# Dilated attention by even and odd query tokens: 128 keys of one parity per dilated group, one PSUM bank per head

## The chip, the cores and the metric

The program runs on one core of one Trainium2 chip. The metric is the device time of one launch in microseconds (us), here the median of three runs.

## The reference

Two layers (DEPTH 2) of a decoder trunk on 256 tokens of width 1024, all in float32. Each layer projects the normed residual with one wide matrix, runs four attention branches (A, B, C, M), gates and mixes them, and ends in an MLP. The change is in branch C, dilated attention with 8 heads of width 64 in three groups:

```python
C_PATTERNS = ((128, 1), (512, 4), (2048, 16))
for g, (win, dil) in enumerate(C_PATTERNS):
    cq, ck, cv = c_parts[3 * g:3 * g + 3]
    qc = apply_rope(rms_norm(cq.reshape(B, S, C_HEADS, C_HD), c_qn[l, g]), cos_h, sin_h)
    kc = apply_rope(rms_norm(ck.reshape(B, S, C_HEADS, C_HD), c_kn[l, g]), cos_h, sin_h)
    o_g, lse_g = dilated_group(qc, kc, vc, win, dil)
wts = jax.nn.softmax(jnp.stack(lses, axis=0), axis=0)
o_c = jnp.einsum('gbsh,gbshd->bshd', wts, jnp.stack(outs, axis=0))
```

In `dilated_group` position t attends t - m*dilation, for m from 0 to window//dilation. In the groups with dilation 4 and 16 an even token therefore sees only even tokens and an odd one only odd tokens. The weighting of the three groups by their denominators is the same as one softmax over the keys of all three.

## The kernel before

Every weight matrix is streamed from HBM in units of up to 256 rows by 512 columns (`unit`). SyncE issues the load into `raw`, ScalarE (ACT) rounds it to `w_hi` (L937), VectorE (DVE) writes the rest to `w_lo` (L1103), and TensorE (PE) does three matmuls for each 128 rows and 128 tokens: L1366, L1367 and L1368. This stream of weight matmuls fills most of PE's time. Everything else is put between them.

The order on each engine comes from a planner. `plan` makes a list of items with costs, needs and a wish for their place (`order`), and `arrange` places them engine by engine. The engines then run their lists in order and wait on semaphores. Four banks of PSUM (`ps_b`) serve all transposes, scores and outputs of attention. An item that needs banks waits until they are empty.

Branch C in the kernel before, for each layer, each block of 128 query tokens (tt 0 and 1) and each pair of heads (`head_steps`):

- scores, L1415: three items, one per group. Each does one float32 matmul for each head of the pair, with the 64 rows of the head's width as contraction and 128 keys (tt 0) or 256 keys (tt 1). The two heads lie in different halves of the rows. Each item takes two banks.
- mask, L1282: one DVE instruction per head and group adds the mask, negates and keeps the running minimum in `part_top` and, for the last group, `neg_top`. A second short instruction reads the minimum out.
- exp, L1051 on ACT, over 384 or 768 elements a row; then reciprocal and scaling on DVE, L1289 and L1290.
- transposes of the probabilities on PE, L1421: 3 blocks of 128 keys per head in tt 0, and 6 in tt 1 (two items of 4 and 2); each item is copied out by ACT (L1025).
- values, L1443: one item per pair, 3 or 6 key blocks for each of the two heads, summed in one bank.

Queries and keys come to `q_c` and `k_c` by PE transposes (L1395) and ACT evictions (L1009). The last of them is the second eviction of group 2's keys, which the first complete set of scores waits for. Values come straight from the projection in PSUM to `v_c` by ACT (L1040, `copyv`). L1068 is the issue of the gate bias loads from ACT's queue. `home_of` gives places in `q_c` and `k_c` that branch B's tokens borrow before branch C needs them.

Of the kernel before, what the change touches and what calls it, by code (L numbers as in the profile page):

```python
# [7 lines left out]
P = 128  # L8
# [23 lines left out]
assert S == 2 * P and all(d == 1 or d * P >= S for d in DILATION)  # L32
# [6 lines left out]
P_RING, PT_RING = {"C": 2, "": 4}, 2  # L39
# [11 lines left out]
        ("C", 0): (P + 2 * S, C_G * P), ("C", 1): (P + 2 * S + C_G * P, C_G * S)}  # L51
MASK_W = P + 2 * S + C_G * (P + S)
# [89 lines left out]
def plan():  # L142
# [4 lines left out]
         "v": 0, "ready": 0, "pv": 0, "osplit": 0,  # L147
# [135 lines left out]
    def turn(source, came, c, m, width, dest, mode="plain", gain=None, l=0, order=None, since=0.0, **k):  # L283
# [18 lines left out]
        lay = left_homes.get(dest, []) if c == 0 else []  # L302
        soon = (axis[0] if order is None else order) - 3.0
        e = item("evict", "ACT", cost, [t] + lay, order=soon, chain="", lay=lay, of=t, dest=dest, mode=mode, gain=gain, c=c, m=m, width=width, l=l)
# [36 lines left out]
    def copy_values(job, dest, factor, takes):  # L341
        v = count("v")
        it = item("copyv", "ACT", 1.3 if factor else 0.6, [job.last, factor_at.get(factor)], job=job, dest=dest, factor=factor, v=v,
                  takes=takes, root=factor_at.get(factor))
        values_at[dest] = it
        if takes:
            job.taken = it
        return it

    values_at = {}  # L350
# [4 lines left out]
    def head_steps(l, branch, hs, tt, heads):  # L355

        sts, masks_of = [], []
        for h in hs:
# [3 lines left out]
            blocks = TT if branch == "M" else tt + 1  # L362
            st = dict(ring=ring, slot=len(mine) % P_RING[ring], s=s, branch=branch, h=h, tt=tt, blocks=blocks,
                      gs=C_G if branch == "C" else 1, l=l, before=mine[-P_RING[ring]] if len(mine) >= P_RING[ring] else None,
# [12 lines left out]
            masks_of.append([])  # L377
        dests = {"A": ("qA", "kA"), "M": ("qM", "kM"), "B": ("qB%d" % (hs[0] // 4), "kB%d" % (hs[0] // 4))}.get(branch)
        for g in range(sts[0]["gs"]):
            ds = dests or ("qC%d" % g, "kC%d" % g)  # L380
            cost = 4 * sts[0]["blocks"] * P / 2400 * (2 if branch == "B" else 1) + (0.25 if branch in "AC" else 0.15)
            sc = item("scores", "PE", cost, [o for d in ds for o, _ in plain_turns[d]], sts=sts, g=g,
                      turns=[t for d in ds for _, t in plain_turns[d]])
            sc.opens = len(sts)
            for d in ds:
                plain_last.setdefault(d, []).append(sc)
            for n_in, st in enumerate(sts):
                before = st["before"]
                mk = item("mask", "DVE", dve_cost(st["blocks"] * P) + 0.15,
                          [sc] + (before["turns"] if before else []) + (held["heads"] if branch == "C" else []),  # L390
                          st=st, g=g, of=sc, at=n_in, e=count("tile"), pv=held["heads"][0] if branch == "C" else None,
                          last_part=masks_of[n_in][-1] if g else None)
                sc.closed_by.append(mk)
                masks_of[n_in].append(mk)
        copies = []
        for st, own in zip(sts, masks_of):
            gs, blocks = st["gs"], st["blocks"]
            ex = item("exp", "ACT", act_cost(gs * blocks * P, 1) + 0.2, [own[-1]], st=st, tile=own[-1])
            nm = item("pnorm", "DVE", 0.2 + dve_cost(gs * blocks * P), [ex], st=st)
            st["turns"] = []  # L400
            free_at = st["pt_before"]["pv"] if st["pt_before"] else None
            for b in range(0, gs * blocks, 4):
                m = min(4, gs * blocks - b)
                pt = item("pturn", "PE", 0.06 + 0.108 * m, [nm], st=st, c=b, m=m)
                pt.opens = 1
                pc = item("pcopy", "ACT", act_cost(m * P), [pt, free_at], chain="pcopy", of=pt, st=st, c=b, m=m, pv=free_at)
                pt.closed_by = [pc]
                st["turns"].append(pt)
                copies.append(pc)
        first, i = sts[0], sts[0]["i"]  # L410
        vs = {"A": ("vA",), "M": ("vM",), "B": ("vB%d" % (first["h"] // 4),)}.get(branch, ("vC0", "vC1", "vC2"))
        pv = item("pv", "PE", 0.22 * first["gs"] * first["blocks"] + 0.2, copies + [values_at[v] for v in vs], sts=sts,
# [53 lines left out]
    for l in range(DEPTH):  # L466
# [22 lines left out]

        aq = w_in(COL["aq"], BW, part=(0, half), fine=l == 0)  # L490
# [6 lines left out]
        copy_values(j, "vC1", "mix", True)  # L497
# [24 lines left out]
        copy_values(j, "vC2", "mix", True)  # L522
# [129 lines left out]
def hybrid_block(nc, x, mem, positions, inv_freq, g_mix, w_in, b_gate, a_qn, a_kn, a_sink, b_qa_norm, b_kva_norm,  # L652
# [32 lines left out]
    with ExitStack() as ctx:  # L685
# [32 lines left out]
        neg_top, part_top = sb("neg_top", [P, TOPS]), sb("part_top", [P, 2, C_G])  # L718
# [25 lines left out]
        prob_c = part(2 * C_G).rearrange("p (i c) -> p i c", i=2)  # L744
        probT_c = part(2 * C_G).rearrange("p (i c) -> p i c", i=2)
# [4 lines left out]
        ang, trig = start[:, 5 * S + 128:5 * S + 128 + TT * FREQ], start[:, 6 * S:6 * S + 2 * TT * FREQ]  # L750
        exps = {b: (prob_c, probT_c) if b == "C" else (prob[:], probT[:]) for b in "ABCM"}
# [4 lines left out]
        values = {"vA": v_a, "vM": v_m, "vC0": v_c[:, 0], "vC1": v_c[:, 1], "vC2": v_c[:, 2]}  # L756
# [17 lines left out]
        prob_scaled = sem("prob_scaled")  # L774
# [25 lines left out]

        def home_of(home):

            place = tok[:, home] if home in (0, 1) else (q_c if home[0] == "q" else k_c)[:, int(home[2])].rearrange("p c s -> p (c s)")
            return place.rearrange("p (t c) -> p t c", t=TT)
# [56 lines left out]
        def _(pool):  # L861
# [21 lines left out]
            for it in placed["POOL"]:  # L883
# [16 lines left out]
                elif it.kind == "selects":  # L900
                    pool.wait_ge(dve_const, 1)
                    chains = []
                    for (branch, tt), (m0, w) in MASK.items():
                        if (branch, tt) == ("B", 0):
                            continue
                        keys = (tt + 1) * P
                        for g in range(w // keys):
                            cut = mask[:, m0 + g * keys:m0 + (g + 1) * keys]
                            chains.append((cut, dict(base=tt * P, pattern=[[-1, keys]], channel_multiplier=1), 0))
                            reach = P - 1 if branch == "A" else P if branch == "C" and g == 0 else S  # L910
                            if reach < (tt + 1) * P - 1:
                                chains.append((cut, dict(base=reach - tt * P, pattern=[[1, keys]], channel_multiplier=-1), 1))
# [8 lines left out]
        def _(act):  # L921
# [7 lines left out]
            for it in placed["ACT"]:  # L929
# [62 lines left out]
                elif it.kind == "evict":  # L992
# [12 lines left out]
                    if a["mode"] == "plain":  # L1005
# [3 lines left out]
                        nc.scalar.activation(plain[a["dest"]][0:wd, c:c + m], src, ACT.Copy, scale=scale).then_inc(bank_free[b], 1)  # L1009
# [9 lines left out]
                elif it.kind == "pcopy":  # L1019
                    t, st, m, c = a["of"], a["st"], a["m"], a["c"]  # L1020
# [4 lines left out]
                    nc.scalar.activation(exps[st["branch"]][1][:, st["pt_slot"], c * P:(c + m) * P], ps_b[:, b, 0:m * P],  # L1025
                                         ACT.Copy).then_inc(bank_free[b], 1)
                elif it.kind == "copyv":
# [9 lines left out]
                    act.wait_ge(root_ready, a["root"].a["q"] + 1)  # L1037
                    of = ps_d[:, j % 2, :, P:2 * P] if dest == "vA" else ps_d[:, j % 2]
                    for tt in range(TT):
                        last = nc.scalar.activation(values[dest][:, tt], of[:, tt], ACT.Copy, scale=factor[a["factor"]][:, tt:tt + 1])  # L1040
                    last.then_inc(v_ready if dest == "vA" else set_free[j % 2], 1)
                elif it.kind == "loadmem":
# [4 lines left out]
                elif it.kind == "exp":  # L1047
                    st = a["st"]
                    act.wait_ge(masked, a["tile"].a["e"] + 1)
                    p = prob_of(st)[:, 0:st["gs"] * st["blocks"] * P + (st["branch"] == "A")]  # L1050
# [37 lines left out]
        def _(dve):  # L1088
# [8 lines left out]
            for it in placed["DVE"]:  # L1097
# [40 lines left out]
                elif it.kind == "masks":  # L1138
                    dve.wait_ge(pool_const, 1)
                    for g, dil in enumerate(DILATION):  # L1140
                        if dil == 1:
                            continue
                        rest = rests[g]
                        link(nc.vector.tensor_scalar(rest, dist, dil - 1, None, ALU.bitwise_and))
                        for tt in range(TT):
                            m0, keys = MASK["C", tt][0], (tt + 1) * P
                            last = nc.vector.tensor_scalar(mask[:, m0 + g * keys:m0 + (g + 1) * keys], rest[:, 0:keys], 0.0, NEG,
                                                           ALU.not_equal, ALU.mult)
                        link(last)
# [103 lines left out]
                elif it.kind == "mask":  # L1253
                    st, g, t = a["st"], a["g"], a["of"]
# [12 lines left out]
                    else:  # L1267
                        m0 = MASK[branch, tt][0] + g * keys
# [7 lines left out]
                    elif g:  # L1276
                        dve.wait_ge(masked, a["last_part"].a["e"] + 1)
                        first = part_top[:, st["s"] % 2, g - 1:g]
                    else:
                        first = -NEG  # L1280
                    top = top_of(st) if g == st["gs"] - 1 else part_top[:, st["s"] % 2, g:g + 1]
                    nc.vector.tensor_tensor_reduce(prob_of(st)[:, g * keys:(g + 1) * keys], ps_b[:, b, 0:keys], cut,  # L1282
                                                   -(1.0 if branch in "AC" else SCALE[branch]), first, ALU.add, ALU.min,
                                                   top).then_inc(masked, 1)
# [188 lines left out]
```

## Time and profile before

| | |
|---|---|
| median of three runs | 1224.99 us (1223.71 to 1227.89) |
| profiled execution | 1222.76 us |
| its span, first to last instruction | 1221.0 us |
| PE busy | 1208.7 us |
| DVE busy | 832.0 us |
| ACT busy | 701.0 us |
| granted TensorE clock | 1.00 |
| bytes moved by DMA | 202.60 MB |

Busy time of PE counts overlapped matmuls once, so it tells that PE had work and not how fast that work went. The cost of an item on PE is read from the chain of waits, in which the pieces follow one another without overlap.

### The profile page before, as it was taken

How to read it: one execution, taken by the hardware profiler on the slowest of the kernel's cores; microseconds unless marked ns; L12 is line 12 of the kernel's file. 1: busy time of each engine (PE TensorE's matmuls, PEld its weight loads, DVE VectorE, ACT ScalarE, POOL GpSimd, SP SyncE). 2: the span in 40 equal slices, each digit the busy share in tenths (PEclk: the TensorE clock that was granted, in tenths of full speed). 3: DMA queues.
4: the chain of work that ended last, by engine and by line, in shares of the span. 5: the costliest groups of instructions: out<-in, count | busy, mean ns of one | idle time of the engine just before them, and what ended most of it. 6: DMA issues, size and time to landing. Idle time of an engine off the chain costs nothing.

```text
span 1221.0 us, 17637 instructions
## 1 busy us (share of the span) xinstructions
PE 1208.7 (99%) x6232; PEld 979.9 (80%) x6232; DVE 832.0 (68%) x1447; ACT 701.0 (57%) x1079; POOL 145.9 (12%) x127
## 2 busy tenths in 40 slices
PE   8999999999999999999999999999999999999998
PEld 7888787777778888888888878877777788888887
DVE  5868889886766764544567688798877667554444
ACT  5666766645554465455566677666555544645553
POOL 5511322210000000000021223322000000000000
PEclk9999999999999999999999999999999999999999
DMA  9655444465447556666656444545545566566563
GB/s 253 192 142 159 138 121 136 137 202 157 146 137 223 176 176 187 188 187 184 192 160 188 136 146 138 140 138 165 163 130 153 158 188 183 174 188 183 181 188 103
DMA packets 111220, 202.60 MB, mean 166 GB/s; under 512 B 10016, under 2 KB 18720, under 8 KB 111136
## 3 DMA queue, kind: packets, MB, share of 16 engines
q1 hardware_dynamic: 106128, 194.64, 53.6%
q10 hardware_dynamic: 4464, 6.82, 1.8%
q8 instruction: 52, 0.85, 0.3%
q0 software_dynamic: 544, 0.03, 0.1%
q14 instruction: 32, 0.26, 0.1%
HBM read 200.41 MB, written 1.05 MB: 165 GB/s over the span
## 4 chain that ended last, share of the span: by engine, by line
PE 97%; DMA 2%; ACT 1%; issue 0%; DVE 0%; ACTq 0%; DVEq 0%
PE ps_d L1366 24%; PE ps_d L1368 22%; PE ps_d L1367 22%; PE ps_b L1366 5%; PE ps_b L1368 5%; PE ps_b L1367 5%; PE ps_b L1415 4%; PE ps_b L1395 4%; PE ps_b L1443 3%; PE ps_b L1421 2%; DMA raw<-in_w_in_dram 1%; DMA early<-in_mem_dram 1%; ACT w_hi L937 0%; ACT k_c L1009 0%; DVE w_lo L1103 0%
## 5 line engine op out<-in xcount | busy, mean ns | idle before, releaser
L1103 DVE TENSOR_TENSOR w_lo<-raw,w_hi 128x1024 fp32r<-128x1024 f32 (+4 forms) x381 | 451.2, 1189 | 277.0 <-ACT w_hi L937 276.0
L937 ACT ACTIVATE w_hi<-raw 128x1024 fp32r<-128x1024 f32 (+4 forms) x381 | 391.3, 1027 | 421.6 <-PE ps_d L1368 315.5
L1366 PE MATMUL ps_d<-w_hi,h_hi 128*128 128x512 f32 (+3 forms) x704 | 283.8, 403 | 1.4 <-DVE w_lo L1103 0.9
L1368 PE MATMUL ps_d<-w_hi,h_lo 128*128 128x512 f32 (+3 forms) x704 | 267.7, 380 | 0.0
L1367 PE MATMUL ps_d<-w_lo,h_hi 128*128 128x512 f32 (+3 forms) x704 | 267.0, 379 | 0.0
L1366 PE MATMUL ps_d<-w_hi,r_hi 128*128 128x512 f32 (+1 forms) x552 | 219.9, 398 | 0.0
L1368 PE MATMUL ps_d<-w_hi,r_lo 128*128 128x512 f32 (+1 forms) x552 | 214.2, 388 | 0.0
L1367 PE MATMUL ps_d<-w_lo,r_hi 128*128 128x512 f32 (+1 forms) x552 | 214.0, 388 | 0.0
L1366 PEld LDWEIGHTS ps_d<-w_hi,h_hi 128*128 128x128 f32 x704 | 132.4, 188 | 33.3 <-issue 10.3
L1368 PEld LDWEIGHTS ps_d<-w_hi,h_lo 128*128 128x128 f32 x704 | 132.2, 188 | 25.2
L1367 PEld LDWEIGHTS ps_d<-w_lo,h_hi 128*128 128x128 f32 x704 | 132.8, 189 | 19.3
L1366 PEld LDWEIGHTS ps_d<-w_hi,r_hi 128*128 128x128 f32 x552 | 103.7, 188 | 23.7 <-issue 3.5
L1368 PEld LDWEIGHTS ps_d<-w_hi,r_lo 128*128 128x128 f32 x552 | 103.6, 188 | 21.2
L889 POOL TENSOR_TENSOR root<-sums,power 128x16 f32<-128x16 f32 (+3 forms) x32 | 86.5, 2702 | 274.6 <-DVE sums L1179 232.2
L1367 PEld LDWEIGHTS ps_d<-w_lo,r_hi 128*128 128x128 f32 x552 | 103.8, 188 | 19.0
L1366 PE MATMUL ps_b<-w_hi,h_hi 128*128 128x512 f32 x256 | 101.1, 395 | 0.0
L1367 PE MATMUL ps_b<-w_lo,h_hi 128*128 128x512 f32 x256 | 99.7, 390 | 0.0
L1368 PE MATMUL ps_b<-w_hi,h_lo 128*128 128x512 f32 x256 | 99.7, 389 | 0.0
L1368 PEld LDWEIGHTS ps_b<-w_hi,h_lo 128*128 128x128 f32 x256 | 48.1, 188 | 10.0
L1366 PEld LDWEIGHTS ps_b<-w_hi,h_hi 128*128 128x128 f32 x256 | 48.1, 188 | 9.9 <-issue 0.5
L1367 PEld LDWEIGHTS ps_b<-w_lo,h_hi 128*128 128x128 f32 x256 | 48.1, 188 | 9.4
L889 POOL TENSOR_TENSOR factor_mlp<-sums,power 128x1 f32<-128x1 f32 x4 | 2.2, 557 | 379.4 <-DVE sums L1188 379.4
(158 smaller groups left out, 1239.9 us busy)
## 6 DMA issues: line engine op xcount, KB each, us to landing
raw<-in_w_in_dram SPq DMA_DIRECT2D x151, 512.0 KB, 3.7
raw<-in_w_up_dram SPq DMA_DIRECT2D x64, 512.0 KB, 3.7
raw<-in_w_down_dram SPq DMA_DIRECT2D x64, 512.0 KB, 4.0
raw<-in_w_branch_dram SPq DMA_DIRECT2D x32, 512.0 KB, 3.7
raw<-in_m_w_kv_dram SPq DMA_DIRECT2D x16, 512.0 KB, 4.5
raw<-in_w_out_dram SPq DMA_DIRECT2D x16, 512.0 KB, 3.7
early<-in_b_gate_dram ACTq DMA_DIRECT2D x16, 256.0 KB, 3.6
raw<-in_w_in_dram SPq DMA_DIRECT2D x8, 384.0 KB, 3.8
```

The source lines that it names most:

```text
L889: nc.gpsimd.tensor_tensor(to, sums[:, slot, 0:w], power[:, 0:w], ALU.pow).then_inc(root_ready, 1)
L937: nc.scalar.activation(w_hi[:, u % RING, 0:kn, 0:cn], raw[:, u % RAW, 0:kn, 0:cn], ACT.Copy).then_inc(hi_split, 1)
L1103: nc.vector.tensor_tensor(w_lo[:, u % RING, 0:kn, 0:cn], raw[:, u % RAW, 0:kn, 0:cn], w_hi[:, u % RING, 0:kn, 0:cn].bitcast(F32), ALU.subt ...
L1366: nc.tensor.matmul(o, hi[:, a["c"], cut], wh, start=a["first"], stop=False)
L1367: nc.tensor.matmul(o, hi[:, a["c"], cut], wl, start=False, stop=False)
L1368: last = nc.tensor.matmul(o, lo[:, a["c"], cut], wh, start=False, stop=a["last"])
L1395: last = nc.tensor.transpose(ps_b[0:wd, b, k * P:(k + 1) * P], v, ident[:])
L1415: nc.tensor.matmul(ps_b[:, b, 0:keys], q, k, start=True, stop=True).then_inc(bank_full[b], 1)
L1421: last = nc.tensor.transpose(ps_b[:, b, k * P:(k + 1) * P], prob_of(st)[:, c * P:(c + 1) * P], ident[:])
L1443: last = nc.tensor.matmul(ps_b[r0:r0 + d, b, c:c + P], v[:, b2, vh * d:(vh + 1) * d], pT[:, k * P:(k + 1) * P], start=k == 0, stop=k == le ...
```

## The change

Query block tt now means the tokens of parity tt: even tokens in the first block, odd tokens in the second.

- The eviction of `q_c` (all groups) and of `k_c` (groups 1 and 2) reads PSUM with a stride of two and writes even tokens first and odd tokens behind (`sides`). Keys of group 0 stay in order of time.
- A head has four blocks of keys in either query block: two for group 0 (all 256 keys) and one for each dilated group (128 keys of its parity). The scores of all three groups are one item, fill one bank (512 columns), and have one mask instruction of 512, one exp of 512, one scaling of 512, one transpose item of four blocks and one copy.
- The three scores items of a pair become one, whose matmuls go group by group and, in a group, head by head.
- Values of groups 1 and 2 have to lie by parity on the partitions. `copyv` writes them to a borrowed place (`q_c` or `k_c` of group 0), and four DMAs from ACT's queue (`vmove`) carry each to `v_c`: 64 partitions of 512 values each. The eviction that next writes the borrowed place waits for them, and so does the first values item of each query block.
- The masks are rebuilt for the new layout, `o_c` is written with a stride of two by `oevict`, and the ring of probabilities of branch C holds 4 heads and not 2.

```diff
-P_RING, PT_RING = {"C": 2, "": 4}, 2
+P_RING, PT_RING = {"C": 4, "": 4}, 2
...
+        if stage:
+            values_at[dest] = moved[stage] = item("vmove", "ACT", 1.5, [(it, 0.3)], job=job, dest=dest, stage=stage, k=count("move"))
...
-            blocks = TT if branch == "M" else tt + 1
+            blocks = {"M": TT, "C": C_BLOCKS}.get(branch, tt + 1)
...
-        for g in range(sts[0]["gs"]):
-            ds = dests or ("qC%d" % g, "kC%d" % g)
...
+        ds = {"A": ("qA", "kA"), "M": ("qM", "kM"), "B": ("qB%d" % (hs[0] // 4), "kB%d" % (hs[0] // 4))}.get(
+            branch, tuple(n_ + "C%d" % g for g in range(C_G) for n_ in "qk"))
...
+                        if a["dest"] in sides:
+                            to, src = sides[a["dest"]][:, c:c + m], src.rearrange("p c (i t) -> p c t i", t=TT)
+                        if a["moved"] is not None:
+                            at = a["moved"].a["k"]
+                            act.wait_ge(v_moved[at % 2], 16 * 2 * TT * (at // 2 + 1))
...
+                elif it.kind == "vmove":
+                    job, g = a["job"], int(a["dest"][2])
+                    act.wait_ge(set_free[job.j % 2], set_value(job))
+                    of = home_of(a["stage"])
+                    for half in range(2):
+                        for tt in range(TT):
+                            act.dma_start(v_c[half * P // 2:(half + 1) * P // 2, g, tt], of[tt::TT, half]).then_inc(v_moved[a["k"] % 2], 16)
...
+                    parts = [(0, slice(0, full))] if branch != "C" else [(0, slice(0, S))] + [(g, qs) for g in range(1, C_G)]
+                    at_col = 0
+                    for g, ks in parts:
+                        wide = ks.stop - ks.start
+                        for st, b in zip(a["sts"], it.banks):
...
+                    if branch == "C":
+                        vs = [v_c[:, 0, t2] for t2 in range(TT)] + [v_c[:, g, tt] for g in range(1, C_G)]
```

PE's order around the first scores of branch C in the first layer, before (`ps_b<-k_c,q_c` are scores, `ps_b<-ident,tok` transposes of queries and keys, `ps_d` weight matmuls; an order row x2 of float32 is four records of the trace):

```order
L1395 MATMUL ps_b<-ident,tok 128x128 [waits tok_ready,masked]
L1395 MATMUL ps_b<-ident,tok 128x128 x3
L1415 MATMUL ps_b<-k_c,q_c 128x128 [waits bank_free1,bank_free0,bank_free3,bank_free2,masked]
L1415 MATMUL ps_b<-k_c,q_c 128x128
L1415 MATMUL ps_b<-k_c,q_c 128x128 [waits bank_free1,bank_free2,bank_free0]
L1415 MATMUL ps_b<-k_c,q_c 128x128
L1366 MATMUL ps_d<-w_hi,h_hi 128x512 [waits lo_split,bank_free0,set_free0]
```

The same place on PE in the changed kernel:

```order
L1414 MATMUL ps_b<-ident,tok 128x128 [waits tok_ready,bank_free1]
L1414 MATMUL ps_b<-ident,tok 128x128 x3
L1438 MATMUL ps_b<-k_c,q_c 128x256 [waits bank_free3,bank_free1,bank_free2,bank_free0]
L1438 MATMUL ps_b<-k_c,q_c 128x256
L1438 MATMUL ps_b<-k_c,q_c 128x128 x4
L1385 MATMUL ps_d<-w_hi,h_hi 128x512 [waits lo_split,bank_free0,set_free0]
```

Before, the scores of groups 0 and 1 of the first pair stood earlier, and here came group 2's and the next pair's first. Now all six matmuls of the first pair stand here, behind the last transpose of keys. The next pair's scores follow 12 weight matmuls later, and the first transposes of probabilities 6 after that:

```order
L1438 MATMUL ps_b<-k_c,q_c 128x256 [waits bank_free3,bank_free1,bank_free2,bank_free0]
L1438 MATMUL ps_b<-k_c,q_c 128x256
L1438 MATMUL ps_b<-k_c,q_c 128x128 x4
L1385 MATMUL ps_d<-w_hi,h_hi 128x512 [waits lo_split,bank_free1]
...
L1446 MATMUL ps_b<-ident,early 128x128 [waits prob_scaled,masked]
L1446 MATMUL ps_b<-ident,early 128x128 x3
```

On ACT, the place where the first values are moved, in the changed kernel (the row with `q_c<-ps_d` is the copy to the borrowed place, the DMA rows are `vmove`):

```order
L1055 ACTIVATE q_c<-ps_d,factor_mix 128x512 [waits root_ready,unit_done]
L1055 ACTIVATE q_c<-ps_d,factor_mix 128x512
L944 ACTIVATE w_hi<-raw 128x1024 [waits unit_done,raw_landed1]
L1063 DMA v_c<-q_c 64x512 [waits set_free0]
L1063 DMA v_c<-q_c 64x512 x3
L944 ACTIVATE w_hi<-raw 128x1024 [waits unit_done,raw_landed2]
```

Before, the two roundings to `w_hi` stood next to each other there; now the four DMA issues lie between them.

## Rows read from the trace of the kernel before

**Rows 1.** The page: busy time by engine, and the chain that ended last by engine.

```profile
PE 1208.7 (99%) x6232; PEld 979.9 (80%) x6232; DVE 832.0 (68%) x1447; ACT 701.0 (57%) x1079; POOL 145.9 (12%) x127
...
PE 97%; DMA 2%; ACT 1%; issue 0%; DVE 0%; ACTq 0%; DVEq 0%
```

**Rows 2.** Waits of PE, whole span: us in total, times, longest.

```profile
PE ps_b L1415 <- ACT k_c L1009: 2.8, 2, 1.4
PE ps_b L1395 <- DMA xs<-in_x_dram: 2.7, 1, 2.7
```

**Rows 3.** Busy time by stage: branch C of either layer, and the stretch of the first move.

```profile
257.00:372.00 115.00, 113.60 (x661) 86.06 (x660) 84.03 (x180) 61.87 (x95) 0.00 (x0) 1.00 0.52 151
860.00:975.00 115.00, 113.60 (x660) 86.13 (x659) 83.85 (x178) 61.88 (x95) 0.00 (x0) 1.00 0.52 151
50.00:60.00 10.00, 10.00 (x66) 8.98 (x65) 7.28 (x12) 8.06 (x14) 0.94 (x3) 1.00 0.87 297
```

**Rows 4.** Chain of waits, query block 0: start, us, what, records.

```profile
259.53 0.83 PE ps_b L1415 x8
260.36 0.43 PE ps_d L1366
...
266.51 0.23 PE ps_d L1368
266.75 0.81 PE ps_b L1443 x12
267.56 0.42 PE ps_b L1415 x4
267.98 0.43 PE ps_d L1366
```

**Rows 5.** Chain of waits, query block 1.

```profile
304.94 1.06 PE ps_b L1415 x8
...
308.94 0.63 PE ps_b L1415 x4
...
313.90 0.66 PE ps_b L1421 x6
...
318.64 1.46 PE ps_b L1443 x24
```

**Rows 6.** PE's groups of branch C, shapes apart: records, busy us, mean ns.

```profile
L1421 PE MATMUL ps_b<-ident,early 128*128 128x128 f32 x144 | 19.9, 272 | 0.0
L1443 PE MATMUL ps_b<-early,v_c 128*64 128x128 f32 x288 | 19.3, 278 | 0.0
L1415 PE MATMUL ps_b<-k_c,q_c 64*128 64x256 f32 x96 | 16.3, 424 | 0.0
L1415 PE MATMUL ps_b<-k_c,q_c 64*128 64x128 f32 x96 | 11.5, 321 | 2.8 <-ACT k_c L1009 2.8
```

**Rows 7.** DVE's groups: masks of 128 and 256, scaling of 768, rounding of weights.

```profile
L1282 DVE CUSTOM_DVE_ANT_0 early<-ps_b,mask 128x256 f32<-128x256 f32 x16 | 6.1, 419 | 0.6 <-PE ps_b L1415 0.6
L1282 DVE CUSTOM_DVE_ANT_0 early<-ps_b,mask 128x128 f32<-128x128 f32 x16 | 4.3, 286 | 3.2 <-PE ps_b L1415 2.9 <-issue 0.3
L1290 DVE TENSOR_SCALAR early<-early,den 128x768 f32<-128x768 f32 x16 | 9.9, 621 | 0.6
L1103 DVE TENSOR_TENSOR w_lo<-raw,w_hi 128x1024 fp32r<-128x1024 f32 x347 | 424.7, 1227 | 257.8 <-ACT w_hi L937 256.8
```

**Rows 8.** ACT's groups: exp of 768, evictions of keys.

```profile
L1051 ACT ACTIVATE early<-early,neg_top 128x768 f32<-128x768 f32 x16 | 14.8, 930 | 3.7 <-DVE neg_top L1282 3.6
L1009 ACT ACTIVATE k_c<-ps_b 128x512 f32<-128x512 f32 x12 | 6.9, 590 | 1.9 <-PE ps_b L1395 1.9
```

**Rows 9.** Issues of the bias loads on ACT's queue (ns min/median/max), and their landing.

```profile
L1068 ACTq DMA_DIRECT2D early<-in_b_gate_dram x16: 334/334/335, 238.6 to 972.5; - x16
...
DMA to landing us min/median/max: 3.0/3.6/5.1
```

**Rows 10.** Where the first move falls, in order of time: ACT, DVE and PE.

```profile
51.67 1.06 ACT L937 ACTIVATE w_hi<-raw 128x1024 fp32r<-128x1024 f32 x1 [0.31 <-DMA raw<-in_m_w_kv_dram]
...
52.77 1.23 DVE L1103 TENSOR_TENSOR w_lo<-raw,w_hi 128x1024 fp32r<-128x1024 f32 x1 [0.15 <-ACT w_hi L937]
...
57.47 0.39 PE L1366 MATMUL ps_d<-w_hi,r_hi 128*128 128x512 f32 x1
```

More of the change, by code:

```diff
@@ L31 @@
 N_IN = COL["gate"] + 4 * D
-assert S == 2 * P and all(d == 1 or d * P >= S for d in DILATION)
+assert S == 2 * P and DILATION[0] == 1 and all(d % TT == 0 and d * P >= S for d in DILATION[1:])
+C_BLOCKS = TT + C_G - 1
 UC, NW = 2, 512
@@ L302, in turn @@
         lay = left_homes.get(dest, []) if c == 0 else []
+        came_from = moved.pop(dest, None)
         soon = (axis[0] if order is None else order) - 3.0
-        e = item("evict", "ACT", cost, [t] + lay, order=soon, chain="", lay=lay, of=t, dest=dest, mode=mode, gain=gain, c=c, m=m, width=width, l=l)
+        e = item("evict", "ACT", cost, [t, (came_from, 3.0) if came_from else None] + lay, order=soon, chain="", lay=lay, moved=came_from, of=t, dest=dest, mode=mode, gain=gain, c=c, m=m, width=width, l=l)
         out = e
@@ L339, in plan, with copy_values @@
     factor_at = {}
[L341 removed]
+    def copy_values(job, dest, factor, takes, stage=None, after=None):
         v = count("v")
[L343 removed]
+        it = item("copyv", "ACT", 1.3 if factor else 0.6, [job.last, factor_at.get(factor), after], job=job, dest=dest, factor=factor, v=v, after=after,
                   takes=takes, root=factor_at.get(factor))
@@ new lines, in head_steps @@
+        ds = {"A": ("qA", "kA"), "M": ("qM", "kM"), "B": ("qB%d" % (hs[0] // 4), "kB%d" % (hs[0] // 4))}.get(
+            branch, tuple(n_ + "C%d" % g for g in range(C_G) for n_ in "qk"))
+        cost = 4 * sts[0]["blocks"] * P / 2400 * (2 if branch == "B" else 1) + (0.25 if branch in "AC" else 0.15)
+        sc = item("scores", "PE", cost, [o for d in ds for o, _ in plain_turns[d]], sts=sts,
+                  turns=[t for d in ds for _, t in plain_turns[d]])
+        sc.opens = len(sts)
+        for d in ds:
+            plain_last.setdefault(d, []).append(sc)
@@ L395, in head_steps @@
+        for n_in, st in enumerate(sts):
+            before = st["before"]
+            mk = item("mask", "DVE", dve_cost(st["blocks"] * P) + 0.15,
+                      [sc] + (before["turns"] if before else []) + (held["heads"] if branch == "C" else []),
+                      st=st, of=sc, at=n_in, e=count("tile"), pv=held["heads"][0] if branch == "C" else None)
+            sc.closed_by.append(mk)
+            masks_of.append(mk)
         copies = []
         for st, own in zip(sts, masks_of):
-            gs, blocks = st["gs"], st["blocks"]
@@ L398, in head_steps @@
-            ex = item("exp", "ACT", act_cost(gs * blocks * P, 1) + 0.2, [own[-1]], st=st, tile=own[-1])
-            nm = item("pnorm", "DVE", 0.2 + dve_cost(gs * blocks * P), [ex], st=st)
+            blocks = st["blocks"]
+            ex = item("exp", "ACT", act_cost(blocks * P, 1) + 0.2, [own], st=st, tile=own)
+            nm = item("pnorm", "DVE", 0.2 + dve_cost(blocks * P), [ex], st=st)
             st["turns"] = []
             free_at = st["pt_before"]["pv"] if st["pt_before"] else None
[L402 to L409, printed above, removed]
+            pt = item("pturn", "PE", 0.06 + 0.108 * blocks, [nm], st=st, m=blocks)
@@ new lines, in _ @@
+                    for k, v in enumerate(vs):
+                        for st in sts:
+                            h = st["h"]
+                            vh, r0, c = h // (A_H // A_KV) if branch == "A" else h, h * d % P, h * d // P * P
+                            pT = exps[branch][1][:, st["pt_slot"]]
+                            last = nc.tensor.matmul(ps_b[r0:r0 + d, b, c:c + P], v[:, vh * d:(vh + 1) * d],
+                                                    pT[:, k * P:(k + 1) * P], start=k == 0, stop=k == blocks - 1)
```

176 lines of the change are left out of this document (85 added, 91 removed).

## The prediction

> **What bounds the kernel now.** I read the page first. PE is busy for 1208.7 of 1221.0 us, and the chain that ended last is PE for 97% [rows 1]. Next the waits of PE. Once the program has started, PE waits for another engine for little more than 2.8 us, twice 1.4 us, before the scores of branch C that need the last eviction of keys [rows 2]. Then the stages. In branch C of either layer PE is busy for 113.6 of 115 us, DVE for 84 and ACT for 62, at clock 1.00 [rows 3]. So the time is the sum of what PE's instructions take one behind the other. A change that takes work from PE shortens the program by just that, as long as no new wait appears; work taken from DVE and ACT is worth nothing by itself. The price of an item on PE is its piece in the chain, where nothing overlaps. The mean durations of the groups overlap (272 ns for a transpose that advances the chain by 0.11) and serve here only for counts.
>
> **Scores.** A pair's item costs 0.42 us with 128 keys [rows 4] and 0.63 with 256 [rows 5]. The counts are 96 records of either width, four to an item, so 24 items of each [rows 6]. Two items of 256 back to back take 1.06, so the second adds only 0.43: the item has about 0.2 us of fixed cost, and then runs at its columns [rows 5]. Before: 24 x 0.42 + 24 x 0.63, less 0.4 for the two pairs of items that follow each other with 256 keys, is 24.8 us. After: 16 items, each with one 256-key part (0.63) and two 128-key parts behind it without a semaphore between. This continuation with 128 keys is not in the trace. From below it costs half of 0.43, or 0.22. The values items say the same: 12 more records add 1.46 - 0.81 = 0.65, or 0.22 per four [rows 4, 5]. From above it costs 0.41, since the one place where two 128-key items stand together took 0.83 [rows 4]. There the second item has waits of its own, and inside the new item there are none, so I take 0.22, and keep 0.41 for the range. After: 16 x (0.63 + 0.44) = 17.1. Gain: 7.7 us.
>
> By the page "TensorE: Matmul & The Clock Gate" of the Trainium skill, section on the mechanism of packing, a load of weights overlaps matmuls in flight only when the row group differs. In the new item the next group's weights go to the same rows as the matmuls before them, so the rule speaks for the upper price. The values items load to all 128 rows each time and still advance by 0.22 per four records [rows 4, 5], against the rule, and this row decides.
>
> **Values.** 8 items of 12 records and 8 of 24, 288 in all [rows 6], take 8 x 0.81 + 8 x 1.46 = 18.2 us [rows 4, 5]. After there are 16 items of 16 records, at 0.81 + 0.22 = 1.03, or 16.4. Gain: 1.7.
>
> **Transposes of probabilities.** 144 records [rows 6] at 0.66 / 6 = 0.11 [rows 5] become 8 x 16 = 128. Gain: 1.8.
>
> **Returns to the weight stream.** A weight matmul takes 0.23 in the chain, but 0.43 right behind scores or values of 64 rows or columns [rows 4]. Behind a transpose it doesn't. In the order of instructions 46 such items of branch C are followed by a weight matmul before, and 32 after (16 scores, 16 values). 14 fewer at 0.20: gain 2.8.
>
> The sum is 7.7 + 1.7 + 1.8 + 2.8 = 14.0 us.
>
> **What costs nothing, and under what cover.** On DVE six masks of a head become two of 512. The step from 128 to 256 adds 133 ns [rows 7], so 512 take about 0.69. The exp of 512 and the scaling of 512 are below the 0.93 and 0.62 of the 768-wide ones [rows 7, 8]. These aren't PE's time; they matter only if transposes come before their probabilities. For the first pair: mask and readout 0.8, exp and readout 0.9, reciprocal and scaling 0.7, handovers 0.3, a rounding of weights in the way 1.23 [rows 7], 3.9 in all. PE has 12 weight matmuls (3.0 with 0.2 for the return), the next pair's scores (1.07) and 6 more (1.6), some 5.6 us, before it wants them. Margin 1.7 us. The initial wait of 1.4 before the first scores stays, because the same last eviction releases them [rows 2]. The evictions now read with a stride of two, which no row shows. I take their 0.59 as it is [rows 8]. At twice that, two of them ahead of the first scores would add 1.2 us in each layer, 2.4 in all. Less than 0.59 I exclude, since the elements stay the same. The masks are built long before the first use, and the strided `oevict` is four instructions.
>
> **The moves of values.** 16 DMAs of 128 KB. An issue holds ACT's queue for 0.33 us [rows 9], so each group of four holds it for 1.3. Queued behind them is the next rounding to `w_hi`, then DVE, then PE. In the first layer this falls where DMA engines are already 0.87 busy with 297 GB/s [rows 3], and 512 KB more are 1.8 us at that rate. The load of weights that follows is rounded at 51.67, its rest is done at 54.00, and PE takes it at 57.47 [rows 10]: 3.5 us of margin against 1.3 + 1.8 = 3.1. So I charge 0. If both add up and the planner's small shifts eat the rest, PE waits up to 1.5 us in each layer. The moved values themselves are wanted more than 30 us after their issue; a bias load lands after 3.6, at most 5.1 [rows 9].
>
> From the profiled execution: 1222.76 - 14.0 = 1208.8. The median of the runs shown is 2.2 higher, from which the same sum gives 1211.0. I take the middle, **1209.8**. A measurement of this kernel tells a difference of about 0.3% (3.7 us) from none.
>
> **The rivals.**
>
> *The short parts of the scores don't run on* (0.41 each, as in [rows 4]). For it: the only pair of 128-key items in the trace, and the rule above. Against it: the values items at the same width. 32 parts cost 0.19 more each, 6.1 us: **1215.9**. Chance 0.12.
>
> *The moves and evictions come through*: PE waits where the moves collide with the weight loads (up to 3.0 in both layers), and the strided evictions lengthen the first wait (up to 2.4). For it: ACT and DMA are full at that place. Against it: the margin of 3.5. About half of both is 2.7: **1212.5**, at most 1215.2. Chance 0.10.
>
> *The gain is eaten*: the new order puts transposes of probabilities ahead of their time, and PE waits 0.4 us before each of the 32 items in the two layers, some 13 us: **1222**, within 0.3%. For it: the margin at DVE is the thinnest there. Against it: no transposes item is in the list of waits now [rows 2], and the worked margin is 1.7. Chance 0.05.
>
> *Slower: the mask of a full bank becomes the bound.* One mask now has to be done before anything of a head goes on, and a pair's second mask stands behind the first. If the 512-wide mask takes much longer than 0.69, PE waits before the transposes of each pair. To lose, the 16 pairs have to give back 14.0 + 3.7 = 17.7 us, 1.1 each, on top of the margin of 1.7. It decides from two masks that take 2.8 us more together, 2.1 us for one. At 2.6 us each the waits are 16 x 2.1 = 34: **1243**. Against it: 286 and 419 ns at 128 and 256 columns are a straight line [rows 7]. Chance 0.03.
>
> **How the numbers follow.** The forecast has 0.70. It and the first two rivals are faster by over 0.3%: 0.92. Within 0.3%: 0.05. Slower: 0.03. The lower end is the forecast from the profiled time less the 2.8 us of first waits that a shifted order could hide: 1206.0. The upper end is the rival of the short parts with one more us of waits: 1217.0. What lies above is 0.08 and a part of the middle cases.
>
> **What would show each step.** In the chain of the changed kernel a scores item of branch C with 12 records is one piece of 1.07 us (1.45 if the rival holds); a values item of 16 records is 1.03; a transposes item of four is 0.44; weight matmuls behind them 0.43. Records: 64 of 256 keys and 128 of 128 keys, 256 for values, 128 for transposes. PE's waits stay below 10 us with 1.4 twice before scores. The mask takes 0.69, the evictions of queries and keys 0.59. PE's busy time is some 14 us lower. Wrong would be: new waits of PE on `prob` scaling or on `w_lo` near 55 and 650 us, scores items above 1.2 us, or a busy time of PE that did not fall.

## The result, and the profile after

| | before | changed |
|---|---|---|
| median | 1224.43 us (1223.71 to 1227.89, 4 runs) | 1210.2 us (1209.3 to 1211.05, 4 runs) |
| ratio | | 0.9878, 95% interval 0.9857 to 0.99 |
| span of the profiled execution | 1221.0 us | 1208.7 us |

The change makes the kernel 14.2 us faster (12.2 to 17.5 by the interval); 14.0 was worked out, and 1209.8 forecast. The page of the profile after the change (busy time by engine, then the chain by engine; before: [rows 1]):

```profile
PE 1196.8 (99%) x6184; PEld 980.9 (81%) x6184; DVE 819.7 (68%) x1319; ACT 694.6 (57%) x1063; POOL 142.6 (12%) x128
...
PE 98%; DMA 1%; ACT 0%; issue 0%; ACTq 0%; DVE 0%
```

PE is as full as it was, and busy for 11.9 us less. PE's waits (before: [rows 2]):

```profile
PE ps_b L1414 <- DMA xs<-in_x_dram: 3.7, 1, 3.7
PE ps_b L1438 <- ACT k_c L1022: 2.8, 2, 1.4
PE ps_d L1357 <- POOL ident L870: 1.6, 1, 1.6
PE ps_d L1385 <- ACT q_c L997: 0.5, 2, 0.3
```

The two waits of 1.4 us before the first scores are still there, as forecast, and no new one came. The chain of waits shows the items of branch C in the first layer (before: [rows 4, 5]; start, us, what, records):

```profile
260.96 1.15 PE ps_b L1438 x12
262.11 0.43 PE ps_d L1385
...
307.53 1.08 PE ps_b L1438 x12
308.61 0.43 PE ps_d L1385
...
314.28 0.44 PE ps_b L1446 x4
...
317.94 1.02 PE ps_b L1473 x16
```

A scores item is one piece of 1.08 us (1.07 forecast; the first of each layer, behind its wait, takes 1.15), a values item 1.02 (1.03), four transposes 0.44 (0.44), and the weight matmul behind scores or values 0.43. PE's groups, shapes apart, give the counts (before: [rows 6]), and DVE's and ACT's the new widths (before: [rows 7, 8]):

```profile
L1446 PE MATMUL ps_b<-ident,early 128*128 128x128 f32 x128 | 17.2, 272 | 0.0
L1473 PE MATMUL ps_b<-early,v_c 128*64 128x128 f32 x256 | 17.5, 279 | 0.0
L1438 PE MATMUL ps_b<-k_c,q_c 64*128 64x256 f32 x64 | 11.2, 427 | 2.8 <-ACT k_c L1022 2.8
L1438 PE MATMUL ps_b<-k_c,q_c 64*128 64x128 f32 x128 | 9.8, 271 | 0.0
```

```profile
L1299 DVE CUSTOM_DVE_ANT_0 early<-ps_b,mask 128x512 f32<-128x512 f32 x32 | 20.8, 687 | 10.3 <-PE ps_b L1438 10.3
```

```profile
L1073 ACT ACTIVATE early<-early,neg_top 128x512 f32<-128x512 f32 x32 | 22.9, 717 | 25.4 <-DVE neg_top L1299 25.4
L1022 ACT ACTIVATE k_c<-ps_b 128x512 f32<-128x512 f32 x12 | 6.9, 589 | 1.9 <-PE ps_b L1414 1.9
L1022 ACT ACTIVATE q_c<-ps_b 128x512 f32<-128x512 f32 x12 | 6.7, 591 | 1.1 <-PE ps_b L1414 1.1
```

The mask takes 687 ns, on the straight line through 286 and 419, and the strided evictions take the same 0.59 us as before. (The row of `k_c` mixes both kinds: only group 0's keys, four of the twelve evictions, are read with a stride of one. The twelve lie between 573 and 600 ns.)

The two profiled spans differ by 12.3 us, not by 14.2, because this execution started later: the first weight matmul begins at 11.40 us before and at 14.76 here (timeline of PE, before first):

```profile
11.40 0.48 PE L1366 MATMUL ps_d<-w_hi,h_hi 128*128 128x512 f32 x1
```

```profile
10.58 1.11 PE L1414 MATMUL ps_b<-ident,xs 128*128 128x128 f32 x4 [3.74 <-DMA xs<-in_x_dram]
11.49 3.62 PE L1357 MATMUL ps_d<-ident 128*128 128x128 f32 x16
14.76 0.78 PE L1385 MATMUL ps_d<-w_hi,h_hi 128*128 128x512 f32 x1
```

Here PE stood idle for the input for 3.74 us and not 2.68, and then its 16 dummy transposes took 3.62 us against 1.91. The granted clock (the number before the last two of each row) tells why: from 10 to 15 us it was 1.00 before and 0.50, the level of 1.2 GHz, in the changed kernel (busy time by stretch, PE first; one row of before, then two of the changed kernel):

```profile
10.00:15.00 5.00, 5.00 (x34) 4.42 (x32) 2.91 (x4) 3.62 (x5) 5.00 (x8) 1.00 1.15 213
```

```profile
5.00:10.00 5.00, 1.84 (x14) 1.60 (x12) 1.83 (x4) 1.36 (x3) 5.00 (x8) 0.90 1.02 312
10.00:15.00 5.00, 4.42 (x21) 4.42 (x22) 2.50 (x5) 3.27 (x5) 5.00 (x8) 0.50 1.17 216
```

The same split runs through all profiled executions. Where the clock stayed at 1.00 in this stretch (before and four of the versions below), the first weight matmul begins between 11.4 and 12.3 us; where it was between 0.50 and 0.70 (the changed kernel and six versions), between 13.1 and 16.7. What decides between the two isn't shown: PE had waited 1.6 to 3.6 us for the input in the first group and 2.6 to 5.9 in the second.

A measure free of the start is the distance between the first scores of branch C in the two layers: 862.42 - 259.53 = 602.89 us before, 856.34 - 260.96 = 595.38 after. That is 7.5 us for one layer, 15.0 for two, 1.0 more than the 14.0 worked out. Of this, 0.5 is a wait of some 0.3 us in each layer that before has and the changed kernel hasn't; the rest is not assigned. It stands in the list of PE's waits before:

```profile
PE ps_b L1443 <- ACT probT L1025: 0.5, 2, 0.3
```

### The profile page after: what moved, and what is told of

Same layout as the page of the kernel before. It is cut to its first block, busy times and chain, and to the rows that moved or that the text cites. A ratio compares the mean times of both kernels' runs of the same rounds, so it can differ in the third digit from the quotient of the medians.

```text
span 1208.7 us, 17209 instructions
## 1 busy us (share of the span) xinstructions
PE 1196.8 (99%) x6184; PEld 980.9 (81%) x6184; DVE 819.7 (68%) x1319; ACT 694.6 (57%) x1063; POOL 142.6 (12%) x128
## 4 chain that ended last, share of the span: by engine, by line
PE 98%; DMA 1%; ACT 0%; issue 0%; ACTq 0%; DVE 0%
PE ps_d L1385 24%; PE ps_d L1386 23%; PE ps_d L1387 23%; PE ps_b L1385 5%; PE ps_b L1386 5%; PE ps_b L1387 5%; PE ps_b L1414 4%; PE ps_b L1438 4%; PE ps_b L1473 3%; PE ps_b L1446 2%; DMA xs<-in_x_dram 1%; PE ps_d L1357 0%; ACT w_hi L944 0%; ACT k_c L1022 0%; ACT q_c L997 0%
## 5 line engine op out<-in xcount | busy, mean ns | idle before, releaser
L892 POOL TENSOR_TENSOR root<-sums,power 128x16 f32<-128x16 f32 (+3 forms) x32 | 83.9, 2622 | 277.0 <-DVE sums L1200 233.2
```

The costliest lines, as they stand in the source:

```text
L892: nc.gpsimd.tensor_tensor(to, sums[:, slot, 0:w], power[:, 0:w], ALU.pow).then_inc(root_ready, 1)
```

## The experiments

The median of before in each batch of runs stands with each ratio, since the batches differ by some tenths of a us.

### Head by head and not group by group

The loop over heads goes outside the loop over groups:

```diff
-                    at_col = 0
-                    for g, ks in parts:
-                        wide = ks.stop - ks.start
-                        for st, b in zip(a["sts"], it.banks):
+                    for st, b in zip(a["sts"], it.banks):
+                        at_col = 0
+                        for g, ks in parts:
+                            wide = ks.stop - ks.start
```

> The changed kernel, with the six matmuls of a scores item in branch C issued head by head (256, 128, 128 keys of the first head, then of the second) and not in turns. My theory: the two heads of a pair run side by side in different halves of the rows only while their matmuls alternate. Head by head, each head's 512 columns take about 0.85 us alone, so an item takes 1.8 to 1.9 us in place of 1.08, and 16 items add 12 to 13 us: about 1223. Rival: TensorE finds the other half of the rows by itself; the item stays at 1.08 and the time at 1210.

Measured: 1218.19 us (1216.41 to 1221.04, 6 runs), 0.9954 of before (0.9938 to 0.9971; before 1224.27). The chain of waits shows two scores items of this version:

```profile
259.65 1.65 PE ps_b L1438 x10
261.30 0.43 PE ps_d L1385
...
264.29 1.61 PE ps_b L1438 x10
```

An item takes 1.61 us in place of 1.08: 16 x 0.53 = 8.5, and the time rose by 8.0. The rival fell, for the order inside an item is worth more than half of the whole gain. My number fell too. I had the two heads run one after the other (1.8 to 1.9 us), but the item takes 0.2 to 0.3 less. The second head may start before the first one's last matmul is done; no row shows it.

### A full-width transpose between the parts

```diff
                         at_col += wide
+                        if branch == "C" and at_col < full:
+                            nc.tensor.transpose(ps_b[:, it.banks[0], at_col:at_col + P], ident[:], ident[:])
```

> The changed kernel, with one transpose of the identity (128 rows, 128 columns) put behind the first and behind the second part of each scores item of branch C, 32 in all, written where the next part overwrites it. My theory: what the merged item saves is mostly the change between 64-row and 128-row matmuls, about 0.15 us on the way out and 0.2 on the way back in. Each transpose then costs 0.11 + 0.35 = 0.46 us and the 32 of them 14.7: about 1225. Rival: a matmul costs its columns and nothing for the change; 32 x 0.11 = 3.5, about 1213.7.

Measured: 1223.79 us (1222.22 to 1225.78, 10 runs), 1.0 of before (0.999 to 1.001; before 1224.27). Thirty-two transposes eat the gain of the change. In the chain an item of this version reads:

```profile
262.77 0.63 PE ps_b L1438 x4
263.40 0.26 PE ps_b L1443
263.66 0.42 PE ps_b L1438 x4
264.08 0.26 PE ps_b L1443
264.34 0.42 PE ps_b L1438 x4
264.76 0.43 PE ps_d L1385
```

A transpose costs 0.26 us here and not 0.11, and the part behind it 0.42 and not 0.22. So each interruption costs 0.15 on the way out of 64 rows and 0.20 on the way in, besides its own work: 32 x (0.26 + 0.20) = 14.7, of which 13.6 were measured. The theory holds; the rival's 1213.7 is out. Nor is it the interruption as such: behind a full-width transpose a weight matmul takes 0.23 in the chain, and behind scores or values 0.43. The page "TensorEngine Tiling (Array Packing)" of the Trainium skill says under Key Properties that a change of the tiling mode drains the engine. The measured price of 0.35 us there and back agrees with such a rule, but the trace shows only the longer pieces, and not what the engine does in them.

### The short parts twice

```diff
                         wide = ks.stop - ks.start
+                        if branch == "C" and g:
+                            for st, b in zip(a["sts"], it.banks):
+                                h = st["h"]
+                                r0 = h % 2 * HD
+                                nc.tensor.matmul(ps_b[:, b, at_col:at_col + wide], q_c[r0:r0 + HD, g, h // 2, qs],
+                                                 k_c[r0:r0 + HD, g, h // 2, ks], start=True, stop=True)
```

> The changed kernel, with the four matmuls of the two dilated groups in each scores item issued twice (the second time over the first). Nothing changes its number of rows, so by my theory each repeated part of 128 keys costs 0.22 us: 32 x 0.22 = 7.1, about 1217.3. Rival (the short parts don't run on, 0.41 each): 32 x 0.41 = 13.1, about 1223.3.

Measured: 1216.65 us (1215.04 to 1217.47, 4 runs), 0.9943 of before (0.9922 to 0.9964; before 1224.27). 6.5 us more than the changed kernel for 32 parts is 0.20 each. The chain has each part as a piece (L1429 is the repetition; the second dilated group follows at the same pace):

```profile
258.91 0.22 PE ps_b L1429 x4
259.13 0.22 PE ps_b L1444 x4
```

This settles the term whose bounds lay widest apart, 0.22 against 0.41. It also bears on the rule that the prediction weighed (the mechanism of packing in "TensorE: Matmul & The Clock Gate" of the Trainium skill): the weights of each part go to the same rows as the part before and still load during its matmuls, against the rule in the form in which the prediction took it. A part's matmuls and the next part's loads, from the timelines of PE and PEld:

```profile
258.94 0.42 PE L1444 MATMUL ps_b<-k_c,q_c 64*128 64x128 f32 x4
259.05 0.34 PEld L1429 LDWEIGHTS ps_b<-k_c,q_c 64*128 64x128 f32 x4
```

### Merging alone, in the kernel before

Where all groups have 128 keys (query block 0), the kernel before gets one scores item and one mask:

```diff
-        for g in range(sts[0]["gs"]):
+        merged = branch == "C" and tt == 0
+        for g in range(1 if merged else sts[0]["gs"]):
...
+                    if a["sts"][0]["merged"]:
+                        for g in range(C_G):
+                            for st, b in zip(a["sts"], it.banks):
+                                h = st["h"]
+                                r0 = h % 2 * HD
+                                last = nc.tensor.matmul(ps_b[:, b, g * P:(g + 1) * P], q_c[r0:r0 + HD, g, h // 2, 0:P],
+                                                        k_c[r0:r0 + HD, g, h // 2, 0:P], start=True, stop=True)
```

> The kernel before, with one part of the change alone: in query block 0, where the three groups have 128 keys each, the scores of a pair's three groups are one item in one bank (384 columns) with one mask. No parity, no moves; keys, values and transposes as before. My theory (merging saves, apart from fewer keys): 24 items of 0.42 us (10.1 in all) become 8 of 0.86 (6.9), and 8 returns to the weight stream at 0.20 go, 4.8 us in all: about 1219.5 against 1224.4 before. Rival: what the change saved comes from fewer keys, and merging alone gives nothing: 1224.

Measured: 1220.09 us (1217.84 to 1220.9, 6 runs), 0.9963 of before (0.9949 to 0.9976; before 1224.27): 4.2 us less, with every key, value and transpose in place. PE's groups have the same 96 records of 128 keys, now 7.5 us busy against 11.5 in [rows 6]:

```profile
L1411 PE MATMUL ps_b<-k_c,q_c 64*128 64x128 f32 x96 | 7.5, 288 | 2.8 <-ACT k_c L1014 2.8
```

### Parity alone, with three items again

```diff
-        cost = 4 * sts[0]["blocks"] * P / 2400 * (2 if branch == "B" else 1) + (0.25 if branch in "AC" else 0.15)
-        sc = item("scores", "PE", cost, [o for d in ds for o, _ in plain_turns[d]], sts=sts,
+        for g in range(C_G if branch == "C" else 1):
+            col, keys = (0, sts[0]["blocks"] * P) if branch != "C" else ((0, S) if g == 0 else (S + (g - 1) * P, P))
+            cost = 4 * keys / 2400 * (2 if branch == "B" else 1) + (0.25 if branch in "AC" else 0.15)
+            sc = item("scores", "PE", cost, [o for d in ds for o, _ in plain_turns[d]], sts=sts, g=g, keys=keys,
...
+                    top = top_of(st) if branch != "C" or g == C_G - 1 else part_top[:, st["s"] % 4, g:g + 1]
```

> The changed kernel with the scores of a pair in three items again (256, 128 and 128 keys), each with its own two banks and its own mask, so parity, moves, transposes and values are those of the change and only the merging is undone. Theory: what is left of the gain is fewer keys: values 1.7, transposes 1.8, scores 24.8 to 16 x 1.47 = 23.5, and 4 fewer returns to the weight stream 0.8, in all 5.6 us: about 1218.5 against 1224 before. Rival: the parity layout brings the whole gain and merging nothing: 1210.

Measured: 1218.37 us (1217.5 to 1220.08, 5 runs), 0.9956 of before (0.9943 to 0.9968; before 1223.74). Fewer keys are worth 5.4 us (5.6 worked out). The remaining 8 to 9 us of the change come from putting the three items into one. The prices account for them: 16 x (0.63 + 0.42 + 0.42 - 1.08) = 6.2 for scores, and 2.0 for the 10 returns between 42 (in this version's order) and 32.

This version also has, far from any wait, what the trace before lacked: two items of 128 keys back to back, each with its own banks and semaphores.

```profile
315.78 0.65 PE ps_b L1448 x8
316.42 0.43 PE ps_d L1395
```

The second adds 0.65 - 0.42 = 0.23. So even separate short items run on, and the 0.83 of [rows 4], right behind a wait, was no price for them. What made it 0.83 isn't shown.

### Without the moves

```diff
-        values = {"vA": v_a, "vM": v_m, "vC0": v_c[:, 0], "vC1": home_of("qC0"), "vC2": home_of("kC0")}
+        values = {"vA": v_a, "vM": v_m, "vC0": v_c[:, 0], "vC1": v_c[:, 1], "vC2": v_c[:, 2]}
...
-        copy_values(j, "vC1", "mix", True, stage="qC0", after=last_c)
+        copy_values(j, "vC1", "mix", True)
```

> The changed kernel without the moves: the values of groups 1 and 2 are written by ScalarE straight to their tile, in order of time, and no DMA carries them (this leaves out the sorting of values by parity). Theory: the 16 DMAs hide behind the margin of the weight stream, 1210 as the changed kernel, within 1 us. Rival: they hold up the rounding of weights near 50 and 650 us, and the time falls by 2 to 3 us.

Measured: 1211.21 us (1207.89 to 1212.55, 4 runs), 0.9891 of before (0.9875 to 0.9907; before 1223.95). This kernel leaves out the sorting of the values and not only the DMAs. The moves cost nothing that can be measured (the interval is about 2 us to either side), and in neither version does PE wait near them, though their issue was dearer than I had it. Here are the issues in the changed kernel (ns min/median/max, then landing), and below them the place of the first move in order of time, on ACT, DVE and PE:

```profile
L1063 ACTq DMA_DIRECT2D v_c<-q_c x8: 483/616/646, 53.4 to 651.2; - x8
L1063 ACTq DMA_DIRECT2D v_c<-k_c x8: 472/618/620, 144.1 to 741.4; - x8
...
DMA to landing us min/median/max: 2.7/3.4/6.0
```

```profile
53.43 2.48 ACTq L1063 DMA_DIRECT2D v_c<-q_c  x4
56.01 1.06 ACT L944 ACTIVATE w_hi<-raw 128x1024 fp32r<-128x1024 f32 x1 [1.53 <-PE ps_d L1387]
...
57.10 1.23 DVE L1125 TENSOR_TENSOR w_lo<-raw,w_hi 128x1024 fp32r<-128x1024 f32 x1 [1.36 <-ACT w_hi L944]
...
60.23 0.39 PE L1385 MATMUL ps_d<-w_hi,r_hi 128*128 128x512 f32 x1
```

Four issues hold ACT's queue for 2.48 us, 0.62 each, against 0.33 for a bias load [rows 9]. (The profile names PE as what ended ACT's idle time before 56.01, but the issues end just there.) For the weights that follow, the rest is done at 58.33, and PE wants it at 60.23: of the 3.5 us of margin [rows 10], 1.9 are left. Other profiled executions have dearer first moves. In five of the other versions one of the four issues took 1.2 to 1.5 us and the four together 3.1 to 3.4; in the four of these with the changed kernel's order, the margin was 1.4 to 1.7. Here is the dearest, of the short parts twice:

```profile
50.31 3.36 ACTq L1063 DMA_DIRECT2D v_c<-q_c  x4
```

Even there PE doesn't wait at this place.

### Plain evictions

```diff
-                            to, src = sides[a["dest"]][:, c:c + m], src.rearrange("p c (i t) -> p c t i", t=TT)
+                            to, src = sides[a["dest"]][:, c:c + m], src.rearrange("p c (t i) -> p c t i", t=TT)
```

> The changed kernel with queries and keys evicted in order of time, so that PSUM is read with a stride of one (this leaves out the sorting of queries and keys by parity). Theory: the strided evictions take the same 0.59 us, and the time stays at 1210. Rival: they are slower and lengthen the two waits before the first scores, and without them the time falls by up to 2.4 us.

Measured: 1210.06 us (1207.57 to 1211.29, 4 runs), 0.9889 of before (0.9872 to 0.9905; before 1223.95). No difference, as the 0.59 us of the strided evictions said already.

### The ring of two

```diff
-P_RING, PT_RING = {"C": 4, "": 4}, 2
+P_RING, PT_RING = {"C": 2, "": 4}, 2
```

> The changed kernel with places for the probabilities of 2 heads of branch C again, and not 4. Theory: the next pair's masks come after the transposes of the pair before in any case, PE's order does not change, and the time stays at 1210. Rival: the ring of 4 lets masks run ahead; with 2, PE waits for transposes, some tenths of a us for each of 16 pairs, 2 to 5 us in all.

Measured: 1209.9 us (1207.95 to 1210.29, 4 runs), 0.9881 of before (0.9866 to 0.9896; before 1223.95). PE's order is the same instruction for instruction, and the time is the same within the noise. The longer ring is no part of the gain.

### A version that beats both: narrow items together

If a return to the weight stream costs 0.2 us, an order with fewer returns must be faster. The planner gets one more rule for PE:

```diff
+def narrow(it):
+    return it.kind in ("scores", "pv") and it.a["sts"][0]["branch"] != "M"
...
                 soon = min(c[0][0] for c in can) + LOOK[e]
-                pick = min((c for c in can if c[0][0] <= soon), key=lambda c: (c[0][1], c[0][0]))
+                near = [c for c in can if c[0][0] <= soon]
+                if e == "PE" and placed[e] and narrow(placed[e][-1]) and any(narrow(c[2]) for c in near):
+                    near = [c for c in near if narrow(c[2])]
+                pick = min(near, key=lambda c: (c[0][1], c[0][0]))
```

> The changed kernel with one more rule in the planner: behind scores or values of 64 or 96 rows or 64 columns, TensorE takes another such item next if one is ready within the 0.1 us it looks ahead. In the order 46 such items are then followed by a weight matmul and not 74. Theory: a return to the weight stream costs 0.2 us, so 28 fewer save 5.6 us: about 1204.6. Rival: the 0.2 us is only the tail of the item and is paid wherever the next one stands; the time stays at 1210. Second rival: items moved ahead of the weight stream leave it late, PE waits, and the time rises.

Measured: **1203.15 us** (1202.2 to 1203.35, 4 runs), 0.9828 of before (0.9813 to 0.9842; before 1223.95). That is 6.8 us less than the version with the ring of two, which is the changed kernel in PE's order and ran in the same batch. All work is the same; only its order differs. The chain of waits shows values and scores back to back, with one return for both:

```profile
266.99 1.02 PE ps_b L1480 x16
268.01 1.08 PE ps_b L1445 x12
269.09 0.43 PE ps_d L1392
...
295.87 1.02 PE ps_b L1480 x16
296.90 1.96 PE ps_b L1445 x24
298.85 0.42 PE ps_d L1392
```

Two scores items together take 1.96 and not 2.16, so they share the fixed cost of the way in too. That is a part of the 1.2 us beyond the 5.6 expected; the rest is within the noise of the two medians.

### Looking further ahead for a partner

```diff
-                soon = min(c[0][0] for c in can) + LOOK[e]
+                soon = min(c[0][0] for c in can) + (0.6 if e == "PE" and placed[e] and narrow(placed[e][-1]) else LOOK[e])
```

> The version with narrow items together, which behind such an item looks 0.6 us ahead for another one and not 0.1. In the order 42 of the 96 narrow items are then followed by a weight matmul, against 46. Theory: 4 fewer returns at 0.2 us save 0.8, and the waits for partners are too short to matter: about 1202.3. Rival: TensorE stands idle for the partner, up to 0.6 us each time, and the time rises to 1204 or more.

Measured: 1204.79 us (1202.41 to 1204.85, 5 runs), 0.9839 of before (0.9826 to 0.9853; before 1223.74). The interval overlaps with that of the version above, so it isn't settled whether this is slower; the 0.8 us that I expected did not show. Counted from the first weight matmul, the profiled execution is 1.3 us longer (1188.7 against 1187.4), which speaks for the rival. Its list of waits has small new ones:

```profile
PE ps_b L1480 <- ACT probT L1045: 0.7, 2, 0.4
PE ps_b L1453 <- ACT q_c L1029: 0.5, 2, 0.2
```

## Why the prediction was right

**Scores, 7.7 us.** The item measured 1.08 us against 1.07 worked out. The term rested on 0.22 us for a 128-key part without a semaphore, which no row before had. The repeated parts measured 0.22 in the chain. The row that spoke for 0.41 (two items of 128 keys back to back at the first scores) stood right behind a wait; such a pair elsewhere took 0.65 and not 0.83.

**Values 1.7, transposes 1.8.** 16 x 1.02 and 128 records at 0.11: as worked out. Together with what fewer keys save in scores and returns when there are three items, the parity layout with its fewer keys measured 5.4 us.

**Returns, 2.8.** The weight matmul at 0.43 behind scores and values, and the transposes put between the parts, confirm that a change of width has a price, 0.20 for the return. The reordered version confirms that it is paid once for a row of narrow items: 28 returns for 6.8 us, with what the scores items save among themselves.

**Costs taken as nothing.** The evictions, the mask and the wait before the first scores came out as forecast. One term was mis-sized: "an issue holds ACT's queue for 0.33 us" was read from 128 rows out of HBM; a move from SBUF to SBUF with 64 partitions took 0.62, so a group of four held the queue for 2.5 us and not 1.3. By the prediction's own sum this would have been too much: 2.5 for the issues and 1.8 for the 512 KB are 4.3 us against 3.5 of margin, a wait of 0.8. The two did not add up. Counted from the first weight matmul, the weights behind the move were rounded 1.0 us later than before and wanted 0.6 earlier, so 1.6 of the margin went. That nothing had to be charged was right for the reason given (the margin), but not by the numbers given, and so partly luck. The term should have had two bounds too, since no row before had a DMA of this kind.

**The rivals.** That the short parts don't run on is out by its direct measurement, and that moves and evictions come through is out by PE's list of waits, with the two versions without them in agreement. The gain eaten by early transposes, and the mask of a full bank as the bound, did not come: PE waits for neither, and the mask takes 687 ns where the second needed 2.1 us.

**The level.** Between the sum from the profiled execution and the sum from the median lay 2.2 us, and I took the middle (1209.9 if added exactly). That was a guess, and it came out at 0.4 us from the median. The record has a reason for the 2.2: the profiled execution before had a mean granted clock of 1.000. Of the 17 executions of before in the first batch, the four at 1.000 took 1221.9 to 1222.6 us and the five at 0.997 took 1224.9 to 1227.1. At 0.997 the median of before is 1225.4 and the changed kernel's two executions took 1211.0: 14.4 us, near the 14.2 of the medians. The profiled span fell by only 12.3 us, because its start took 3.4 us longer, most of it at the lower clock, and by that clock PE's busy time fell by 11.9 and not by the 14 forecast: the 16 dummy transposes alone were busy for 1.7 us more. Whoever had judged the change by the two spans would have missed 2 us of the gain.

## What to carry to other kernels

Where TensorE is the bound and hardly waits, price each kind of item by its piece in the chain of waits, with the piece that follows it: here 64-row items cost 0.2 us to enter and 0.2 to leave, as much as 128 keys for two heads. So merge narrow items, alternate the heads inside them, and put those that remain next to each other; the order alone was worth another 6.8 us. The 16 DMAs that sort values by parity cost nothing here, since the engines that wait for them are not the bound; to count on that in another kernel, read the margin from rows and bound the price of the new work from both sides.

## What the runs showed of the hardware that I had not expected

- An issue of a DMA from SBUF to SBUF over 64 partitions held ACT's queue for 0.62 us (0.47 to 0.65 in the changed kernel, single ones up to 1.5 in others), and one of a bias load for 0.33.
- Two heads' matmuls in different halves of the rows took 1.08 us in turns and 1.61 head by head, where 1.8 to 1.9 was worked out for heads that don't overlap at all.
- The start of the program varies by up to 5 us from one profiled execution to the next (first weight matmul between 11.4 and 16.7 us), more than most terms that were studied here. It goes with the granted clock: up to 12.3 us where it was 1.00 from 10 to 15 us, and from 13.1 where it was 0.50 to 0.70.
